# A hybrid encoder step: the first softmax within the projections, and the order of ACT's weight casts among the experts

## The chip, the cores and the metric

The kernel runs on one core of one Trainium2 chip, as one program and one launch. The metric is the device time in microseconds (us). The core has five engines that run side by side and wait for each other through semaphores: TensorE (PE, matmuls), VectorE (DVE), ScalarE (ACT), GpSimd (POOL) and SyncE (SP, which here only issues DMAs). Each executes its own instructions strictly in order.

## The reference, cut to what matters

One layer of a streaming encoder, in float32, for 1024 prompt frames with 16 meta tokens ahead and 8 samples of 16 frames:

```python
h = rms_norm(x)
z_pool, q, k, v, qi, ki, wi, ga, gb = split(h @ w_in)        # q, k, qi, ki are rotated
score  = sum_h(relu(qi @ ki.T) * wi)                          # the 256 best keys of each query are kept
logits = (q @ k.T) * HEAD_DIM ** -0.5, masked to those keys
o = softmax(logits) @ v                                       # 8 heads, 2 key heads, 4 query heads on each
x = x + (sigmoid(ga) * pool_branch(z_pool) + sigmoid(gb) * (o @ w_attn_out)) @ w_out
h = rms_norm(x)
# 32 experts in 4 groups; each token goes to 2 experts of one group
act = silu(h @ w_g[e]) * (h @ w_u[e])
x = x + sum_e(comb[e] * (act @ w_d[e]))
y = rms_norm(x)
```

## The kernel before, in words

**Numbers in two parts.** Most products are made from a high part (the cast of a float32 to the faster type, made by ACT) and a rest (number minus high part, made by DVE or POOL). Three products, high by high, high by rest and rest by high, stand for one float32 product.

**Projections.** The columns of w_in are taken in 19 pieces (`PIECES`), each staged by SP, cast by ACT (`split_hi`), its rest made by POOL or DVE (`split_lo`). The last four pieces are the queries. They are done by `nat_run(RUN_Q)` (PE L923, ACT L1399, POOL further on): 36 tiles of 128 tokens by 256 columns. Turn i of that loop projects tile i on PE (`proj_nat`, 24 products), ACT copies it out (L1338), POOL rotates it, and three turns later (`LAG`) PE transposes it (`trans`, L917) and ACT copies it into `qT` (L1396). PE uses banks 0 to 3 for projections and 4 and 5 for transposes. Meanwhile DVE picks the 256 best keys (`rounds`, L1795 and L1800) and writes the mask; semaphore `selected` tells of it.

**Attention.** The prompt's groups `PG` are 8 query tiles by 2 key heads, the longest first: `PG[0]` is tile 7 with key head 0, `PG[1]` the same tile with key head 1. A group has 4 heads; each head's logits are made in up to three chunks (`qk`, three products of up to 348 columns, L1004, L1007 and L1010, into bank n % 3). DVE takes a chunk, adds the mask and keeps the maximum (`ttr`, L1837), reduces the chunks' maxima (L1842, L1846), ACT takes the exponential (`expo`, L1502), DVE divides by the sum (`scale`, L1850 and L1852). Then PE transposes the probabilities (`p_trans`, L1032), ACT copies them out (`tevac`, L1512), and PE multiplies by the values (`p_values`, L1045). Step st of the loop over `STEPS` (-1 to 15) transposes and multiplies group st while it makes the logits of group st + 1. `plan(st)` sets which chunks stand between which transposes. Step -1 is the logits and softmax of `PG[0]` alone. Before it, PE, ACT and DVE wait for all projections (`pj_done`, `tr_evac`), ACT casts the first queries (L1528) and the keys of both key heads (L1535, six casts), DVE makes the rests of key head 0 and POOL those of key head 1 (L2284).

From step 6 on each step also holds one of the 8 samples: its logits end step st, and step st + 1 ends with `s_values`: five transposes of its probabilities (L1058, L1061), two copies out by ACT (L1514, L1516) and 20 products (L1070).

**Experts.** SP loads the weights of expert e (gate, up, down, 512 KB each, `load_e`, L784 to L786) into one of 7 slots; from expert 7 on it waits until expert e - 7 has left its slot (`dn_done`). Experts 4 to 6 are loaded behind a wait for the first gathered rows (`hg_in[0]`), and behind them SP stores and reads back a small overflow table (L809 to L813). POOL gathers each expert's rows (L2308) three experts ahead and scatters the results (L2313). For each expert PE does: `gate_up_split(e)` (L1238 to L1242), `e_trans(e + 1)` (L1210), `down_of(e - 1)` (L1223), `turn_act(e)` (L1248). ACT does: `silu_e` (L1625), `rows_upper(e + 1)` (L1639), `expert_upper(e + 2)` (two casts of weights, L1631 and L1632, behind a wait for the weights), the copy of the turned product `actT` (L1666), `second_half(e - 1)` (half of the results, L1646). DVE does: the product `act_rows` (L2051), `rows_lower(e + 1)` (L2035), `first_half(e - 1)` (L2042), `expert_lower(e + 2)` (L2028).

## Time and profile before

| | us |
|---|---|
| median of 3 runs (1361.68 to 1365.5) | 1362.36 |
| the profiled execution, its own time | 1362.2 |
| its span in the profile | 1360.2 |
| PE busy / DVE busy / ACT busy / POOL busy | 1280.9 / 925.5 / 500.7 / 478.8 |
| last query projection ends | 611.7 |
| first transposes of probabilities | 629.3 |
| attention's steps end, output projections begin | about 854 |
| experts, from the first transposes of rows to the last results | 1113 to 1311 |

Times inside the execution are counted from the start of the span. A busy share is no measure of what an engine costs: it has to be read where the next step waits.

### The profile page before, as it was taken

The numbers are of one execution on the slowest core, as the hardware profiler recorded it, in microseconds if no ns is written. First come the engines' busy times: TensorE is split into PE (matmuls) and PEld (weight loads), VectorE is DVE, ScalarE is ACT, GpSimd is POOL, SyncE is SP. The second block draws the span as 40 slices with busy tenths as digits, with TensorE's granted clock in tenths as the row PEclk, the third lists the DMA queues.
The fourth block names the chain that finished last, engine by engine and source line by source line (L and its number), as shares of the span: only waits on it lengthen the run. The fifth ranks groups of instructions, "written<-read, shape, count | busy, mean of one in ns | idle before, by whom it ended". The sixth has DMA issues, their size and how long they took to land.

```text
span 1360.2 us, 21285 instructions
## 1 busy us (share of the span) xinstructions
PE 1280.9 (94%) x7533; PEld 1100.8 (81%) x7533; DVE 925.5 (68%) x2189; ACT 500.7 (37%) x1071; POOL 478.8 (35%) x766
## 2 busy tenths in 40 slices
PE   5999999999989999997999989999999979999986
PEld 5999999999979999996666656999788848777742
DVE  5665888888999989816767656233565658767736
ACT  5654222122121122225556444100322237666533
POOL 5801595778882127541000000120011233333314
PEclk9999999999999999998999999899999989999998
DMA  7201232222213222003000220844321248999857
GB/s 254 72 24 44 87 75 78 39 74 57 63 58 113 66 91 56 2 1 98 1 16 1 66 73 25 291 150 163 124 78 49 77 170 335 351 343 341 302 198 311
DMA packets 79312, 163.78 MB, mean 120 GB/s; under 512 B 12529, under 2 KB 47937, under 8 KB 78065
## 3 DMA queue, kind: packets, MB, share of 16 engines
q1 hardware_dynamic: 65121, 129.31, 27.8%
q0 software_dynamic: 12656, 27.62, 6.1%
q10 hardware_dynamic: 1440, 5.58, 1.0%
q8 instruction: 60, 0.98, 0.3%
q14 instruction: 35, 0.29, 0.1%
HBM read 137.81 MB, written 39.21 MB: 130 GB/s over the span
## 4 chain that ended last, share of the span: by engine, by line
PE 77%; DMA 8%; POOL 5%; DVE 3%; ACT 3%; issue 2%; SPq 0%; ACTq 0%; POOLq 0%; DVEq 0%
PE bank L845 11%; PE bank L844 11%; PE bank L846 11%; PE bank L1045 5%; DMA region_h<-in_wd 4%; PE bank L1116 3%; PE bank L1110 3%; PE bank L1032 3%; PE bank L969 2%; PE bank L1128 2%; PE bank L1127 2%; PE bank L1129 2%; PE bank L1223 2%; DMA region_w<-in_wd 2%; PE bank L1112 2%
## 5 line engine op out<-in xcount | busy, mean ns | idle before, releaser
L1795 DVE MAX8 small<-region_kv 128x8 f32<-128x272 f32 (+4 forms) x241 | 190.2, 828 | 47.6 <-DVE region_kv L1800 47.5
L844 PE MATMUL bank<-h_hi,w_hi 128*128 128x384 f32 (+1 forms) x576 | 196.2, 341 | 0.0
L845 PE MATMUL bank<-h_lo,w_hi 128*128 128x384 f32 (+1 forms) x576 | 196.1, 340 | 0.0
L1800 DVE MATCH_REPLACE8 region_kv<-small,region_kv 128x272 f32<-128x272 f32 (+4 forms) x241 | 195.5, 818 | 0.0
L846 PE MATMUL bank<-h_hi,w_lo 128*128 128x384 f32 (+1 forms) x576 | 194.5, 338 | 0.0
L2116 POOL TENSOR_TENSOR w_lo<-w_stage,w_hi 128x512 fp32r<-128x512 f32 x64 | 80.8, 1295 | 144.7 <-ACT w_hi L1327 144.6
L844 PE MATMUL bank<-w_hi,h_hi 128*128 128x256 f32 x448 | 129.2, 288 | 2.3 <-ACT region_q L1390 2.3
L846 PE MATMUL bank<-w_hi,h_lo 128*128 128x256 f32 x448 | 125.9, 281 | 0.0
L845 PE MATMUL bank<-w_lo,h_hi 128*128 128x256 f32 x448 | 125.9, 281 | 0.0
L846 PEld LDWEIGHTS bank<-h_hi,w_lo 128*128 128x128 f32 x576 | 108.8, 189 | 0.0
L845 PEld LDWEIGHTS bank<-h_lo,w_hi 128*128 128x128 f32 x576 | 108.2, 188 | 0.6
L844 PEld LDWEIGHTS bank<-h_hi,w_hi 128*128 128x128 f32 x576 | 108.0, 188 | 0.5
L1045 PE MATMUL bank<-region_t,region_kv 128*128 128x512 f32 (+1 forms) x176 | 88.0, 605 | 2.4 <-ACT region_t L1512 2.4
L844 PEld LDWEIGHTS bank<-w_hi,h_hi 128*128 128x128 f32 x448 | 84.2, 188 | 2.6 <-ACT region_q L1390 2.5
L846 PEld LDWEIGHTS bank<-w_hi,h_lo 128*128 128x128 f32 x448 | 84.4, 189 | 0.0
L845 PEld LDWEIGHTS bank<-w_lo,h_hi 128*128 128x128 f32 x448 | 84.4, 188 | 0.0
L1484 ACT ACTIVATE region_q<-bank 128x384 f32<-128x384 f32 x48 | 23.6, 492 | 159.6 <-PE bank L846 159.6
L2313 POOL DMA_INDIRECT expert_rows_scratch<-region_t,small_i x32 | 35.2, 1100 | 120.9 <-ACT region_t L1646 85.0
L2275 POOL COPY region_h<-region_q 128x128 f32<-128x128 f32 x8 | 2.4, 294 | 190.9 <-PE bank L1070 190.9
L1116 PE MATMUL bank<-o_hi,wao_lo 128*128 128x384 f32 x192 | 69.0, 359 | 0.0
L1110 PE MATMUL bank<-o_hi,wao_hi 128*128 128x384 f32 x192 | 66.2, 345 | 1.5 <-DVE o_lo_prompt L1867 1.5
L1512 ACT COPY region_t<-bank 128x512 f32<-128x512 f32 (+1 forms) x88 | 50.0, 575 | 47.8 <-PE bank L1032 47.8
(307 smaller groups left out, 3179.5 us busy)
## 6 DMA issues: line engine op xcount, KB each, us to landing
w_stage<-in_w_in SPq DMA_DIRECT2D x72, 256.0 KB, 3.2
region_kv<-in_xa SPq DMA_DIRECT2D x16, 512.0 KB, 5.8
region_q<-in_wg SPq DMA_DIRECT2D x12, 512.0 KB
region_q<-in_wu SPq DMA_DIRECT2D x12, 512.0 KB
region_q<-in_wd SPq DMA_DIRECT2D x12, 512.0 KB
region_w<-in_wg SPq DMA_DIRECT2D x10, 512.0 KB
region_w<-in_wu SPq DMA_DIRECT2D x10, 512.0 KB
region_w<-in_wd SPq DMA_DIRECT2D x10, 512.0 KB
```

What stands on the lines that cost most here:

```text
L844: mm(out, st_hi(k), mv_hi(k), start=(k == 0), stop=False)
L845: mm(out, st_hi(k), mv_lo(k), start=False, stop=False)
L846: last = mm(out, st_lo(k), mv_hi(k), start=False, stop=(k == KD - 1))
L1032: last = nc.tensor.transpose(bank[3 + t % 2][0:rows, r * P:(r + 1) * P], probs_of(x, r)[:, k0:k0 + rows], ident)
L1045: last = mm(bank[5 + slot_of(x)][:, :], vS[0:rows, j, g * HD:(g + 1) * HD], PT[0:rows, t % 3, :], start=(j == 0), stop=(j == nb - 1))
L1110: mm(out, hi, o_hi[:, k, c0:c1], start=(k == 0), stop=False, skip_group_check=True)
L1116: last = mm(out, lo, o_hi[:, k, c0:c1], start=False, stop=(k == KD - 1), skip_group_check=True)
L1512: cp(PT[0:rows, t % 3, :], bank[3 + t % 2][0:rows, :]).then_inc(a_te, 1)
L1795: nc.vector.max(m8[:, q, :], x).then_inc(dve_c, 1)
L1800: nc.vector.match_replace(x, m8[:, q, :], x, TAKEN).then_inc(dve_c, 1)
L2116: tt(w_lo(n)[:, kk * m:kk * (m + 1), :], stage(s if s < KD else s % 4, kk, wd), w_hi(n)[:, kk * m:kk * (m + 1), :].bitcast(F32), ALU.subtr ...
L2313: pool.indirect_dma_start(out=y_d, out_offset=bass.IndirectOffsetOnAxis(ap=idx, axis=0), in_=src, in_offset=None, bounds_check=2 * TOK - 1 ...
```

## The change

Five edits:

1. The logits, softmax and casts of `PG[0]` move from step -1 into `nat_run(RUN_Q)`. PE makes two chunks after each of turns 31 to 36, of which turn 35 holds the last projection. ACT casts in turn 29 and takes the four exponentials in turns 33, 34, 36 and 37. DVE starts as soon as its selection is done. Since the memory of the key and query parts still holds projection data, `PG[0]` has buffers of its own, and its logits use banks 6 and 7 in turn (two, not three). The keys of head 1 are cast in turn 36, after the last projection, and those of head 0 are copied to their lasting place in step 0 (three more copies on ACT).
2. The counts of `qk_high` move with it (`high_at`).
3. The samples' transposes are taken out of `s_values` and put before the last two `p_values` of the step (`s_trans`).
4. Among the experts ACT's `expert_upper(e + 2)` stands behind the copy of `actT` and `second_half(e - 1)`.
5. SP no longer waits for `hg_in[0]` before it loads experts 4 to 6.

```diff
@@ SP
             sp.dma_start(heads[:, :, :], lists[0:P, :, :]).then_inc(lidx_in, 16)
-            sp.wait_ge(hg_in[0], 16)
             for e in range(4, NSLOT):
                 load_e(e)
@@ banks, buffers and turns
+        PB_FIRST = [RW[:, 4096 + 1040 * r:4096 + 1040 * (r + 1)] for r in range(3)] + [RW[:, 0:1040]]
+        def logits_bank(x, n):
+            return bank[6 + n % 2] if x == PG[0] else bank[n % 3]
+        FIRST_AT = {31 + j: [(q // 3, q % 3) for q in (2 * j, 2 * j + 1)] for j in range(6)}
@@ PE, nat_run
                     if i >= LAG:
                         trans(run[i - LAG])
+                    if first is not None:
+                        for q, m in FIRST_AT.get(i, []):
+                            first(PG[0], q, m)
@@ PE, qk
-                if n >= 3:
+                if x == PG[0]:
+                    if n >= 2:
+                        pe.wait_ge(a_sm, n - 1)
+                elif n >= 3:
                     pe.wait_ge(a_sm, n - 2)
@@ PE, the samples
+            def s_trans(x, part):
+                pb, t = probs_of(x, 0), T_AT[x]
+                if part == 0:
+                    pe.wait_ge(a_p, U_AT[x] + 1)
+                    pe.wait_ge(a_te, t - 1)
+                    for j in range(4):
+                        last = nc.tensor.transpose(bank[3 + t % 2][:, j * P:(j + 1) * P], pb[:, j * P:(j + 1) * P], ident)
+                    last.then_inc(a_t, 1)
+                else:
+                    pe.wait_ge(a_te, t)
+                    nc.tensor.transpose(bank[3 + (t + 1) % 2][0:32, 0:P], pb[:, 512:SK], ident).then_inc(a_t, 1)
@@ PE, the steps
+            nat_run(RUN_Q, qk)
...
-            for st in STEPS:
+            for st in STEPS[1:]:
...
                 for j in range(max(nb - 2, 0), nb):
+                    if st - 1 in S_STEP:
+                        s_trans(S_STEP[st - 1], j - (nb - 2))
                     p_values(PG[st], j)
@@ ACT
-            act.wait_ge(pj_done, NU)
+            def first_group_steps(i):
+                if i == 29:
+                    act.wait_ge(w_lo_done, W_AT[NPC])
+                    act.wait_ge(pj_done, W_LAST[NPC - 2])
+                    act.wait_ge(tr_evac, RI["q", 1, 9] + 1)
+                    q_upper(PG[0])
+                    for m, (c0, c1) in enumerate(KEY_CHUNKS):
+                        cp(k_hi_first[m][:, :], kT[:, 0, c0:c1]).then_inc(qk_high, 1)
+                if i in (33, 34, 36, 37):
+                    expo(PG[0], (33, 34, 36, 37).index(i))
+                if i == 36:
+                    act.wait_ge(pj_done, NU)
+                    for c0, c1 in KEY_CHUNKS:
+                        cp(k_hi[:, 1, c0:c1], kT[:, 1, c0:c1]).then_inc(qk_high, 1)
+                if i == 37:
+                    act.wait_ge(tr_evac, RI["q", 3, 8] + 1)
+                    q_upper(PG[1])
+
+            nat_run(RUN_Q, first_group_steps)
             act.wait_ge(tr_evac, len(ROPED))
...
                     tevac(PG[st], j)
+                    if st == 0 and j == 3:
+                        for m, (c0, c1) in enumerate(KEY_CHUNKS):
+                            cp(k_hi[:, 0, c0:c1], k_hi_first[m][:, :]).then_inc(qk_high, 1)
@@ ACT, experts
                 if e + 1 < NE:
                     rows_upper(e + 1)
-                if e + 2 < NE:
-                    expert_upper(e + 2)
                 act.wait_ge(act_turned, e + 1)
                 if e >= 2:
                     act.wait_ge(dn_done, e - 1)
                 cp(actT[:, e % 2, :], bank[6 + e % 2][:, 2 * P:3 * P]).then_inc(actT_ready, 1)
                 if e >= 1:
                     second_half(e - 1)
+                if e + 2 < NE:
+                    expert_upper(e + 2)
@@ DVE
-            dve.wait_ge(pj_done, NU)
-            nc.vector.memset(zero, 0.0).then_inc(zero_ready, 1)
-            dve.wait_ge(zero_ready, 1)
             dve.wait_ge(selected, NT)
+            dve.wait_ge(w_lo_done, W_AT[NPC])
+            dve.wait_ge(pj_done, W_LAST[NPC - 2])
...
-            for st in STEPS:
+            for r in range(REP):
+                ttr(PG[0], r)
+                if r >= 1:
+                    scale(PG[0], r - 1)
+            scale(PG[0], REP - 1)
+            dve.wait_ge(pj_done, NU)
+            nc.vector.memset(zero, 0.0).then_inc(zero_ready, 1)
+            dve.wait_ge(zero_ready, 1)
+            q_rest(PG[1])
+            for st in STEPS[1:]:
```

## Rows read from the trace of the kernel before

**Rows 1.** Stage of experts: PE, PEld, DVE, ACT, POOL, clock, DMA share, GB/s
```profile
1184.00:1311.00 127.00, 117.22 (x731) 90.65 (x730) 86.11 (x117) 76.60 (x139) 38.73 (x39) 1.00 0.81 297
```

**Rows 2.** Timeline of PE, 611 to 632: start, us, engine, line, operation
```profile
611.38 0.28 PE L846 MATMUL bank<-w_hi,h_lo 128*128 128x256 f32 x1
...
617.22 0.32 PE L1004 MATMUL bank<-keys_hi,queries_hi 128*128 128x344 f32 x1
617.38 0.32 PE L1007 MATMUL bank<-keys_hi,o_hi 128*128 128x344 f32 x1
...
618.93 0.49 PE L1004 MATMUL bank<-keys_hi,queries_hi 128*128 128x348 f32 x1
...
629.27 1.02 PE L1032 MATMUL bank<-consts,region_t 128*16 128x128 f32 x4 [4.41 <-DVE region_t L1852]
```

**Rows 3.** Timeline of ACT, 611 to 632
```profile
615.08 2.39 ACT L1535 CAST keys_hi<-region_kv 128x348 fp32r<-128x348 f32 x6
...
618.00 1.28 ACT L1502 ACT_TABLE_LOAD   x1
...
626.96 1.16 ACT L1502 ACTIVATE region_t<-region_t,small 128x1040 f32<-128x1040 f32 x1 [1.30 <-DVE small L1846]
```

**Rows 4.** Timeline of DVE, 602 to 632
```profile
611.79 0.28 DVE L1871 MEMSET region_h<- 128x272 f32 x1 [26.19 <-PE bank L846]
...
626.03 0.51 DVE L1837 CUSTOM_DVE_ANT_0 region_t<-bank,region_kv 128x344 f32<-128x344 f32 x1
...
628.45 0.76 DVE L1852 TENSOR_SCALAR region_t<-region_t,small 128x1040 f32<-128x1040 f32 x1
```

**Rows 5.** Granted clock after the gap, in 2 us windows (columns as in Rows 1)
```profile
634.00:636.00 2.00, 2.00 (x9) 1.17 (x7) 1.11 (x6) 0.78 (x2) 0.00 (x0) 0.81 0.03 8
```

**Rows 6.** Timeline of POOL, 611 to 632
```profile
617.16 2.71 POOL L2284 TENSOR_TENSOR keys_lo<-region_kv,keys_hi 128x348 fp32r<-128x348 f32 x3 [3.59 <-ACT keys_hi L1535]
```

**Rows 7.** Waits of PE, 612 to 1100: total us, times, longest
```profile
PE bank L1070 <- ACT region_t L1516: 6.8, 8, 1.2
```

**Rows 8.** Timeline of PE in a step with a sample
```profile
794.30 1.13 PE L1045 MATMUL bank<-region_t,region_kv 128*128 128x512 f32 x2 [1.38 <-ACT region_t L1512]
```

**Rows 9.** Issues of SP, 1088 to 1300: start, us taken, line
```profile
1112.48 0.33 SPq L784 DMA_DIRECT2D region_q<-in_wg  x1
...
1133.38 0.36 SPq L784 DMA_DIRECT2D region_w<-in_wg  x1
```

**Rows 10.** Waits of SP's queue, 1080 to 1320
```profile
SPq L812 <- DMA overflow_table_scratch<-small_i: 13.8, 1, 13.8
...
SPq L784 <- DMA region_t<-ffn_input_scratch,small_i: 8.5, 1, 8.5
```

**Rows 11.** Timeline of POOL, 1088 to 1130: the first gather
```profile
1107.18 1.93 POOL L2308 DMA_INDIRECT region_t<-ffn_input_scratch,small_i  x1 [4.69 <-DVE small_i L2019]
```

**Rows 12.** Chain that ended last, 1085 to 1190: start, us, what
```profile
1135.04 10.31 DMA region_t<-ffn_input_scratch,small_i
```

**Rows 13.** DMA share behind the overflow table (columns as in Rows 1)
```profile
1130.00:1135.00 5.00, 5.00 (x37) 4.27 (x36) 4.03 (x6) 3.43 (x7) 1.98 (x2) 1.00 0.55 143
```

**Rows 14.** Timeline of DVE among the experts
```profile
1151.54 0.29 DVE L2051 TENSOR_TENSOR region_t<-region_t,bank 128x128 f32<-128x128 f32 x1 [0.27 <-ACT region_t L1625]
...
1154.49 2.35 DVE L2028 TENSOR_TENSOR expert_rest<-region_h,expert_high 128x1024 fp32r<-128x1024 f32 x2
1157.11 0.29 DVE L2051 TENSOR_TENSOR region_t<-region_t,bank 128x128 f32<-128x128 f32 x1 [0.27 <-ACT region_t L1625]
```

**Rows 15.** Timeline of ACT among the experts
```profile
1178.49 1.05 ACT L1631 CAST expert_high<-region_q 128x1024 fp32r<-128x1024 f32 x1 [3.05 <-DMA region_q<-in_wd]
...
1298.09 1.05 ACT L1631 CAST expert_high<-region_w 128x1024 fp32r<-128x1024 f32 x1 [1.59 <-DMA region_w<-in_wd]
```

**Rows 16.** Timeline of PE among the experts
```profile
1180.70 1.98 PE L1223 MATMUL bank<-region_w,region_t 128*128 128x512 f32 x4 [0.67 <-ACT region_t L1666]
...
1182.62 0.35 PE L1238 MATMUL bank<-expert_high,rowsT_hi 128*128 128x256 f32 x1
```

More of the change, by code:

```diff
@@ L183, in build @@
             e_high[0] = slots_w.enter_context(nc.sbuf_tensor("expert_high0", [P, 2, KD, P], F32R))
+        with ExitStack() as first_group:
+            first_group.enter_context(nc.sbuf_tensor("first_probs", [P, 1040], F32))
+            q_hi_first = first_group.enter_context(nc.sbuf_tensor("first_queries_hi", [P, REP, P], F32R))
+            k_hi_first = [None] * 2 + [first_group.enter_context(nc.sbuf_tensor("first_keys_hi2", [P, 344], F32R))]
+            first_group.enter_context(nc.sbuf_tensor("first_more_probs", [P, 7216 - 1896], F32))
+            for m in range(2):
+                k_hi_first[m] = first_group.enter_context(nc.sbuf_tensor(f"first_keys_hi{m}", [P, 348], F32R))
         RW = sb("region_w", [P, 8192])
@@ L485, in high_at @@
         def high_at(n):
-            return 1 if n == 0 else 2 * len(KEY_CHUNKS) + n + 1
+            return [1, 2 * len(KEY_CHUNKS) + 2][n] if n < 2 else 3 * len(KEY_CHUNKS) + n + 1
         def rest_at(n):
@@ L918, in trans, with nat_run @@
                 last.then_inc(tr_done, 1)
-            def nat_run(run):
+            def nat_run(run, first=None):
                 for i in range(len(run) + LAG):
@@ L1003, in qk @@
                         pe.wait_ge(qk_high, 3 * nq + m + 2)
-                    mm(out, qh[:, r, :], k_hi[:, g, c0:c1], start=True, stop=False)
+                    keys = k_hi[:, g, c0:c1] if nq else k_hi_first[m][:, :]
+                    mm(out, qh[:, r, :], keys, start=True, stop=False)
                     if r == 0 and m == 0:
                         pe.wait_ge(qk_low, rest_at(nq))
-                    mm(out, lo, k_hi[:, g, c0:c1], start=False, stop=False)
+                    mm(out, lo, keys, start=False, stop=False)
                     if nq < KVH and r == 0:
@@ L1048, in p_values @@
                     last.then_inc(a_o, 1)
[L1050 to L1061 removed]
+            def s_trans(x, part):
[9 more added lines that the diff above has]
+                    nc.tensor.transpose(bank[3 + (t + 1) % 2][0:32, 0:P], pb[:, 512:SK], ident).then_inc(a_t, 1)
+            def s_values(x):
+                i, t, ob = x[1], T_AT[x], bank[7]
                 if i >= 1:
@@ L1397, in evac_tr, with nat_run @@
                        bk[:, 0:256].rearrange("p (j t) -> p j t", j=2)).then_inc(tr_evac, 1)
-            def nat_run(run):
+            def nat_run(run, first=None):
                 for i in range(len(run) + LAG):
@@ L1407, in nat_run @@
                         evac_tr(run[i - LAG])
+                    if first is not None:
+                        first(i)
             def relus(s0, s1):
@@ L1836, in ttr @@
                     add = sc[i][:, c0:c1] if kind == "p" else zero[:, 0:c1 - c0]
-                    nc.vector.tensor_tensor_reduce(out=probs_of(x, r)[:, c0:c1], in0=bank[n % 3][:, 0:c1 - c0], in1=add,
+                    nc.vector.tensor_tensor_reduce(out=probs_of(x, r)[:, c0:c1], in0=logits_bank(x, n)[:, 0:c1 - c0], in1=add,
                                                    scale=1.0, scalar=MASKED, op0=ALU.add, op1=ALU.max,
```

27 lines of the change are left out of this document (6 added, 21 removed).

## The prediction

> **What bounds the kernel now.** I read the busy shares by stage first. PE does nearly all there is to wait for: what the change can win lies where PE is idle or where something else sets its pace. Three such places are touched.
>
> The first is the change-over from projections to attention. In the timeline of PE the last query product starts at 611.38 and ends at 611.66, and the first transposes of probabilities start at 629.27, behind a wait of 4.41 us for DVE [rows 2]. The reader is to see that in these 17.6 us PE only makes the 12 chunks of the first group. The rest is a chain: casts on ACT, a table load, four rounds of maximum, exponential and division [rows 3, 4].
>
> The second are the samples: eight times PE waits for ACT between a sample's transposes and its products, 6.8 us in all [rows 7].
>
> The third is the expert stage. DVE's products of two experts stand 5.57 us apart where nothing is late [rows 14], but from about 1178 on ACT's cast waits for weights every time, and the casts of experts 12 and 31 are 119.6 us apart [rows 15]: 19 steps, 6.29 us each. PE is busy for 117 of 127 us, the 16 DMA engines move 297 GB/s with a tail in which nothing is loaded [rows 1]. So late weights, not PE, set this pace.
>
> **Part 1, the first softmax: 7.4 us.** A chunk is three products that start 0.16 us apart at the full clock [rows 2], 0.48 us. Turns 31 to 34 hold eight chunks, so the last projection ends 3.8 us later, at 615.5; call it T. The other four follow it. After T: two transposes (some 0.2 us), chunk 8 done at T + 0.7, chunk 9 at T + 1.2. DVE takes chunk 8 (0.5), needs 0.4 from its last chunk to the maximum (from 626.03, the chunk's 0.51 us included, to ACT's exponential at 626.96 it is 0.93) [rows 3, 4], divides head 1 (0.9) and takes chunk 9 only then, to T + 3.1. With two banks, chunk 11 has to wait for that: done at T + 3.6, its maximum at T + 4.55. The exponential and the division behind it took from 626.96 to 629.21 [rows 3, 4], 2.3 us. So PE's first transposes start at T + 6.9 = 622.4 in place of 629.27: **6.9 us**.
>
> On ACT this order holds: head 2's exponential (to T + 3.0), three casts of the second keys (half of 2.39 us [rows 3], to T + 4.2), the last exponential at T + 4.55. The table load of 1.28 us [rows 3] falls into turn 33; PE's four banks and the three turns of lag cover it, and if they did not it would cost its 1.3 us. DVE was idle for 26.19 us before 611.79 [rows 4], so its selection ended at 585.6, before turn 29: nothing new waits for it. The three extra copies in step 0 (1.2 us of ACT) stand behind one copy out, in a step where a turn of PE takes over 2 us; without that cover they would cost 1.2.
>
> Then the clock. The matmuls at 618.93 take 0.49 us in place of 0.32 [rows 2], and after the idle stretch PE works at 1.2 GHz until about 635.2, as the granted 0.81 of the window 634 to 636 shows [rows 5]. That is 5.9 us at half rate, some 2.9 us lost. The new gap is shorter but not empty: PE works for about 1 of the 5 us before its restart. Bounds: nothing regained, or all 2.9. I take 1.0, nearer to the end that the drop at 618 shows, which came after less than 5 us of such idling.
>
> What is late next: POOL's rests of the second keys, which still start when the last transpose is out and take 2.71 us for three [rows 6]. They were ready before PE; now PE needs them one by one within that time: 0.5 us lost (0 to 1.5). DVE's memset of 0.28 us [rows 4] and the query rests end at the same time. Sum: 6.9 + 1.0 - 0.5 = 7.4, bounds 5.5 and 9.3.
>
> **Part 2, the samples: 5.7 us.** Two value products of 0.5 us and more now stand between the transposes and the products that need them, so ACT's copies are hidden. In six of the eight steps the wait stood directly behind the transposes: 6 x 0.8 = 4.8. In two steps PE also waits before the value products (1.38 us at 794.30 [rows 8]); the first transposes fit into that, 0.45 each. In the other two steps ACT's own last exponential ends last, and nothing is won. The later steps hang on a chain of DVE and ACT, but that starts at the sample's logits, which PE makes after these products, so it moves up as a whole. Bounds: 2.4 (three long steps alone) and 7.7.
>
> **Part 3, SP's wait: 2.2 us.** SP waited 8.5 us for the first rows and loaded experts 4 to 6 from 1112.48; then it waited 13.8 us for the overflow table's store, which stood behind that load in its queue, so expert 7 was loaded at 1133.38 [rows 9, 10], though its slot came free at about 1125.6. Meanwhile the DMA engines were busy for 0.55 of the time at 143 GB/s [rows 13]. Now loads 4 to 6 start 8.4 us earlier, the table is through before slot 0 is free, and load 7 starts 7.8 us earlier. Of these 7.8 us the gathers and scatters that had the engines for themselves take some 2.6; **5.2** remain, if the rest of the stage stays bound by weights.
>
> Against this stands the first gather, issued at 1107.18 + 1.93 [rows 11] and landed at about 1112.4: 3.3 us without company. The nearest row with company, a gather issued behind loads of three experts, took 10.31 us [rows 12], which would put everything behind it 6.4 to 7 us later. But that one had a scatter ahead of it in its own queue, this one has nothing. I take 3.0 (0.5 to 6.4). 5.2 - 3.0 = 2.2, bounds -1.2 and 4.7.
>
> The Trainium skill ("DMA: Bandwidth & Descriptors", section "Queues, rings and completion order") says that each DMA engine takes turns between its queues, a packet at a time, so that a lone gather should not sit behind a whole backlog. By that rule the delay would be near the low bound; the row speaks for the high one, and no row shows the lone case.
>
> **Part 4, ACT's order: 0.7 us.** With late weights, arriving at t, the two casts, the copy and the half result went before PE's down product: cast at 1178.49, down at 1180.70, next gate product at 1182.62 [rows 15, 16], t + 4.1. Now the down product no longer waits; the gate product waits for casts (1.05 each), DVE's second rest (half of 2.35 [rows 14]) and its product, t + 3.8. The slot comes free 0.9 us earlier. In a stage bound by weights this counts once, at the end, 0.4; I add 0.3 for fuller queues. Bounds -1 and 2.5. Where nothing is late the casts end 2.3 us later and DVE's next product 1.1 later; it had about 2 us until PE turns it, so 0.9 is left.
>
> **Sum.** 7.4 + 5.7 + 2.2 + 0.7 = 16.0. The profiled execution took 1362.2 (span 1360.2 and 2.0 around it), the median of the runs is 1362.36. 1362.2 - 16.0 = **1346.2**.
>
> **Rivals.**
> - *The queues and the clock are kind* (0.20): the gather is late by 0.5 only, +2.5, and the clock comes back at once, +1.9: 1341.8. For it: the skill's rule above. Against: the dropped clock after a similar gap.
> - *The first rows are late* (0.18): the gather takes 10.3 us as in [rows 12], part 3 gives -1.2: 1349.6.
> - *The chains of ACT and DVE keep the samples' gain* (0.12): part 2 gives 2.4, and half-rate matmuls last as long as before, part 1 gives 6.4: 1350.5.
> - *Slower: the casts come too late on DVE* (0.04). Place: DVE's product of each expert, now behind rests that wait for the later casts. The slack of 0.9 us was worked out, not seen. Each expert that overruns it by x costs x, 31 times; from x = 0.5 on the change is slower than before. At 0.7: 1346.9 + 21.7 = 1368.6. Against: DVE works for 4.7 of 5.57 us.
> - *The turns don't do what they say* (0.02): if the new waits held the first chunks back until the projections are over, part 1 would shrink to 1: 1352.6.
>
> **Numbers.** My forecast, within 3 us, has 0.44. The range takes in the kind and the late case and the samples' one: 1340 to 1353. A measurement of this kernel tells 0.3%, 4.1 us, from no change. Faster by over that: 0.95; within: 0.02; slower: 0.03.
>
> **What would show it.** Last projection ends near 615.5, first probabilities transposed near 622.4, clock below 1.0 for under 5 us behind it. No wait of PE before L1070 except in two steps. SP's load of expert 7 issued near 1126 to 1129 and the first rows landed at 1115 or so, counted without the gain ahead of them. Last weights cast some 15 us earlier than 1298.09. The forecast is wrong if PE stalls in the last turns of the projections, if the experts' pace where nothing is late is above 5.57, or if the first gate product comes over 5 us late.

## The result and the profile after

The changed kernel takes 1354.16 us in the median of 6 runs (1351.77 to 1357.88), the kernel before 1362.69 (1361.68 to 1365.5). The ratio is 0.9939, with a 95% interval of 0.9922 to 0.9955: 8.3 us faster, where 16.0 were forecast. The direction was right, the size was not, and the time lies 1.2 us above the range. The profiled execution of the changed kernel is one of its slower ones, 1357.17 us with a span of 1355.3, so its trace shows a little less gain than the median.

All lines of code are numbered by the kernel that a row comes from. PE in the changed kernel, around the last projections (start, us, engine, line, operation, idle time before and its releaser):

```profile
615.98 0.38 PE L932 MATMUL bank<-consts,nbuf 128*128 128x128 f32 x2
...
619.14 0.43 PE L1024 MATMUL bank<-first_keys_hi,first_queries_hi 128*128 128x344 f32 x1 [0.93 <-DVE small L1880]
...
623.25 1.01 PE L1052 MATMUL bank<-consts,region_w 128*16 128x128 f32 x4 [2.93 <-DVE region_w L1895]
...
624.83 0.66 PE L1027 MATMUL bank<-keys_hi,o_hi 128*128 128x348 f32 x1 [0.28 <-DVE o_hi L1920]
```

The last query product ends at 616.14, so T of the forecast is 616.1 (the projections of this execution began 0.65 us later than before). The first transposes stand at 623.25, T + 7.1, where T + 6.9 was forecast, in place of 629.27 [rows 2]. The stall of 0.93 is the one that was forecast for chunk 11 with two banks, and the last 0.28 is a rest of DVE that took 1.35 us beside POOL's rests.

The waits of PE between there and the experts, in total us, times and longest (answers to [rows 7, 8]):

```profile
PE bank L1094 <- ACT region_t L1543: 1.7, 2, 0.9
...
PE bank L1081 <- ACT region_t L1539: 1.3, 2, 0.9
```

The sample's products waited 6.8 us in eight steps and now wait 1.7 in two. But look at the clock there. Windows of the changed kernel; the columns are the busy times of PE, weight loads, DVE, ACT, POOL, then the granted clock, the DMA share and GB/s:

```profile
812.00:816.00 4.00, 4.00 (x19) 2.44 (x20) 1.38 (x5) 0.00 (x0) 0.00 (x0) 0.58 0.00 0
...
840.00:844.00 4.00, 4.00 (x5) 0.96 (x4) 0.00 (x0) 0.58 (x1) 0.00 (x0) 0.50 0.00 0
844.00:848.00 4.00, 2.49 (x9) 2.45 (x9) 1.38 (x2) 0.00 (x0) 0.00 (x0) 0.50 0.33 78
```

0.50 is the level of 1.2 GHz, half of what PE has at 1.00. Twice the missing share, added over the 4 us windows from 612 to 872, gives the time at the lower level: 20.4 us before, 27.2 after. Before, 4.8 of the 20.4 lay in the gap at 616 to 629 and 0.8 in the wait ahead of the output product at 854, where they cost little (in the gap DVE waited twice for chunks of PE, 0.67 us in all). The other 14.8 us lay in work: 8.9 in the steps (629.3 to 634.8, and at 825) and 5.9 in the output projections, as this window of the kernel before shows:

```profile
856.00:860.00 4.00, 4.00 (x14) 4.00 (x14) 0.00 (x0) 2.04 (x2) 1.19 (x1) 0.50 0.99 344
```

After, 3.3 of the 27.2 lie in waits and 23.9 in work.

Then the start of the experts. The timeline of PE in the changed kernel (in these rows a group is cut where the stretch asked for ends):

```profile
1090.27 15.07 PE L1225 MATMUL bank<-consts 128*128 128x512 f32 x28
1107.45 0.74 PE L1237 MATMUL bank<-consts,region_t 128*128 128x128 f32 x5 [2.11 <-DMA region_t<-ffn_input_scratch,small_i]
```

The issues of SP in it:

```profile
1095.11 0.43 SPq L800 DMA_DIRECT2D region_q<-in_wg  x1
...
1100.29 0.65 SPq L824 DMA_DIRECT2D overflow_table_scratch<-small_i  x1
...
1115.36 0.21 SPq L827 DMA_DIRECT2D nbuf<-overflow_table_scratch  x1
...
1121.36 0.37 SPq L800 DMA_DIRECT2D region_w<-in_wg  x1
```

And the first gather in its chain of waits:

```profile
1098.41 8.90 DMA region_t<-ffn_input_scratch,small_i
```

The loads of experts 4 to 6 stand ahead of the gather, as meant. The gather lands 8.90 us after its issue begins, where it was some 5.2 (1107.18 to about 1112.4, [rows 9, 11]); the warming products no longer cover it, and PE is idle for 2.11 us. The overflow table's store still keeps SP for 14 us, and expert 7 is loaded 31.1 us after the start of the warming products, where it was 34.2. The DMA engines run dry behind the early loads (last three columns: clock, share, GB/s):

```profile
1110.00:1115.00 5.00, 4.95 (x31) 4.70 (x30) 0.31 (x2) 1.36 (x4) 0.28 (x1) 0.70 0.46 175
1115.00:1120.00 5.00, 4.38 (x34) 4.17 (x35) 4.11 (x6) 3.60 (x7) 0.99 (x1) 1.00 0.25 65
```

Among the experts, the stage of [rows 1] in the changed kernel:

```profile
1184.00:1311.00 127.00, 116.67 (x706) 88.01 (x704) 81.31 (x111) 74.00 (x130) 44.09 (x38) 1.00 0.79 289
```

The largest wait of PE there:

```profile
PE bank L1275 <- DVE region_t L2102: 9.9, 12, 1.6
```

A late expert on DVE:

```profile
1193.35 2.36 DVE L2079 TENSOR_TENSOR expert_rest<-region_h,expert_high 128x1024 fp32r<-128x1024 f32 x2 [2.85 <-ACT expert_high L1674]
1195.63 0.28 DVE L2102 TENSOR_TENSOR region_t<-region_t,bank 128x128 f32<-128x128 f32 x1
```

And on PE:

```profile
1195.96 0.33 PE L1275 MATMUL bank<-consts,region_t 128*128 128x128 f32 x1 [1.36 <-DVE region_t L2102]
```

DVE's product of an expert stands behind both rests of the next expert, and these wait for the late casts; PE waits for that product before its turn. The last cast [rows 15] comes at 1293.12, 5.0 earlier and not 15.

Where the time went, in one profiled execution of each kernel (us; "between" runs from the first transposes of probabilities to the first output product, "output" from there to the start of the warming products, "head" from there to the first expert's turn, "experts" from the turn of expert 0 to that of expert 31). These executions lie anywhere in the spread of their kernels' times, so their sums are not the medians.

| | first transposes | between | output | head | experts |
|---|---|---|---|---|---|
| before | 629.3 | 224.7 | 245.2 | 19.4 | 188.4 |
| changed | 623.2 | 222.3 | 244.7 | 24.4 | 187.0 |
| first softmax alone | 621.2 | 230.1 | 242.6 | 20.6 | 187.2 |
| samples alone | 631.3 | 221.6 | 245.1 | 20.8 | 186.9 |
| loads alone | 630.8 | 224.7 | 245.2 | 25.3 | 185.9 |
| casts alone | 629.1 | 224.7 | 245.2 | 19.3 | 187.9 |
| changed, no early loads | 622.0 | 218.9 | 241.9 | 20.0 | 188.5 |
| changed, casts as before | 624.4 | 222.3 | 244.8 | 24.4 | 185.7 |
| first softmax and samples | 622.5 | 222.3 | 244.7 | 20.6 | 187.6 |
| changed, samples as before | 623.6 | 232.8 | 244.0 | 24.0 | 186.6 |
| changed, softmax as before | 630.9 | 221.7 | 245.1 | 27.1 | 186.4 |

### The profile page after: what moved, and what is told of

Read it like the earlier page. It is cut to its first block, busy times and chain, and to the rows that moved or that the text cites. A ratio compares the mean times of both kernels' runs of the same rounds, so it can differ in the third digit from the quotient of the medians.

```text
span 1355.3 us, 21293 instructions
## 1 busy us (share of the span) xinstructions
PE 1284.8 (95%) x7533; PEld 1102.7 (81%) x7533; DVE 927.1 (68%) x2189; ACT 505.0 (37%) x1074; POOL 490.2 (36%) x766
## 4 chain that ended last, share of the span: by engine, by line
PE 78%; DMA 8%; POOL 5%; DVE 3%; ACT 3%; SPq 1%; issue 1%; ACTq 0%; POOLq 0%; DVEq 0%
PE bank L860 11%; PE bank L859 11%; PE bank L861 11%; PE bank L1065 5%; DMA region_w<-in_wd 3%; PE bank L1143 3%; PE bank L1052 3%; PE bank L1137 3%; PE bank L987 2%; PE bank L1154 2%; PE bank L1155 2%; PE bank L1156 2%; PE bank L1250 2%; DMA region_h<-in_wd 2%; PE bank L1139 2%; PE bank L1094 2%
## 5 line engine op out<-in xcount | busy, mean ns | idle before, releaser
L1065 PE MATMUL bank<-region_t,region_kv 128*128 128x512 f32 (+1 forms) x176 | 91.0, 614 | 0.0
L1265 PE MATMUL bank<-expert_high,rowsT_hi 128*128 128x256 f32 x256 | 66.2, 295 | 1.5 <-ACT rowsT_hi L1682 1.5
```

Of the source, the lines that this page charges most:

```text
L1065: last = mm(bank[5 + slot_of(x)][:, :], vS[0:rows, j, g * HD:(g + 1) * HD], PT[0:rows, t % 3, :], start=(j == 0), stop=(j == nb - 1))
L1265: mm(out, rowsT_hi[:, par, k, :], high[:, :, k, :], start=(k == 0), stop=False, skip_group_check=True)
```

## The experiments

My theory after the trace: the two parts at the attention are worth what was forecast less what the clock takes, and the early loads cost more at the first gather than they bring. The rivals: the later casts are the loss, or the DMA rate bounds the experts and makes loads and casts worth nothing either way.

**Each part alone.** On the kernel before, first the softmax's move (all that the diff has on it), then the samples' transposes before the last value products of the step, then SP's wait:

```diff
             sp.dma_start(heads[:, :, :], lists[0:P, :, :]).then_inc(lidx_in, 16)
-            sp.wait_ge(hg_in[0], 16)
             for e in range(4, NSLOT):
```

and ACT's order, `expert_upper(e + 2)` moved behind `second_half(e - 1)`.

> The kernel before with the first softmax within the query projections, and nothing else of the change. My prediction's step 1 prices it at 7.4 us (6.9 of tail, 1.0 of clock, less 0.5 for POOL's rests): ratio 0.9946, some 1355.0 us. The changed kernel's first probabilities were transposed at 623.25, 7.1 us after the end of its last query product, so the tail is as forecast. Rival: the half clock that went from 629:635 comes back in the first steps with samples, where the changed kernel's trace has 812:816 at 0.58; then the output product (854.00 before) starts only 3 to 5 us earlier and the ratio is 0.997.

> The kernel before with the samples' transposes dealt before the last value products of the step before, and nothing else. Step 2 prices it at 5.7 us (six steps at 0.8, two at 0.45): ratio 0.9958, some 1356.7 us. Rival, from the changed kernel's trace: the waits of 0.8 us go, but the clock in the steps with samples falls to 0.50 to 0.58 for eight or more us more than before, which costs 2 to 4 us of the gain: ratio 0.997 to 0.999.

> The kernel before with SP's wait for the first gathered rows taken away ahead of the loads of experts 4 to 7, and nothing else. Step 3 prices it at 2.2 us (5.2 for the earlier load of expert 7, less 3.0 for a later first gather): ratio 0.9984. Theory after the changed kernel's trace: the first gather takes 8.9 us where it took about 5, TensorE idles about 2 us and runs the first expert at half clock, so the first turn of the first expert comes about 5 us later against the start of the stage; the loads of experts 8 on come some 8 to 12 us earlier but the DMA rate of 4 to 7 is shared with them. If only the first expert matters: ratio 1.000 to 1.003. If the loads that come earlier shorten the late experts by 5.2: 0.9984.

> The kernel before with ScalarE's cast of the weights of expert e+2 behind the turned product's copy and the second half, and nothing else. Step 4 prices it at 0.7 us: ratio 0.9995. Theory after the changed kernel's trace: TensorE's turn now waits for DVE's product (9.9 us in 12 waits) because the second rest of the weights stands ahead of it in DVE's order and waits for the later cast; where the casts pace the experts this is 0.8 to 1.5 us in each of up to 12 experts, partly in place of the 6.3 us that the wait for the turned copy cost: between 0 and +4 us, ratio 1.000 to 1.003. If the order pays as meant: ratio 0.996 to 0.9995, and the wait for the turned copy (6.3 us in 11) goes.

Measured: the first softmax 0.9977 (0.9965 to 0.9989), 3.1 us; the samples 0.9965 (0.9951 to 0.9978), 4.8 us; the loads 1.0011 (0.9998 to 1.0023), 1.5 us slower, which the interval does not quite part from nothing; the casts 1.0014 (0.9995 to 1.0033), nothing that can be told. The early loads are not worth 2.2 us here; in their trace the head is 6.0 us longer and the experts 2.5 shorter. PE's first transposes of gathered rows with the loads alone:

```profile
1117.76 1.94 PE L1209 MATMUL bank<-consts,region_t 128*128 128x128 f32 x8 [3.30 <-DMA region_t<-ffn_input_scratch,small_i]
```

The window behind them (columns as above):

```profile
1120.00:1125.00 5.00, 4.54 (x24) 4.57 (x25) 0.88 (x2) 1.60 (x2) 0.99 (x1) 0.57 0.48 178
```

SP's issue of the load of expert 7:

```profile
1132.67 0.37 SPq L784 DMA_DIRECT2D region_w<-in_wg  x1
```

PE is idle for 3.30 us, then runs at the lower clock, and expert 7 is loaded at 1132.67, where it was 1133.38 [rows 9]. The forecast had it 7.8 us earlier: it left out that slot 0 comes free only when the late first expert is done.

The first softmax alone starts the transposes 8.1 us earlier, keeps 2.7 of them at the output product and has 5.3 at the warming products. Its clock fell at 761, 795 and 823, in full work, 2 to 3 us behind stalls of 0.81, 0.81 and 0.86 us. The kernel before has the same three stalls at 766, 797 and 823; its clock held behind the first two and fell behind the third. PE with the first softmax alone, at the first of them:

```profile
759.30 0.96 PE L1091 MATMUL bank<-region_t,region_h 128*128 128x64 f32 x7 [0.81 <-ACT region_t L1538]
```

The windows behind it:

```profile
760.00:764.00 4.00, 4.00 (x22) 2.53 (x21) 0.58 (x2) 0.00 (x0) 0.45 (x2) 0.69 0.18 15
764.00:768.00 4.00, 4.00 (x15) 2.77 (x15) 1.75 (x8) 1.30 (x3) 0.00 (x0) 0.50 0.82 262
```

It has 20.6 us at the lower level, as many as before (20.4), but all of them in the steps, where the kernel before has 8.9: "between" is 5.4 longer. In return its output projections start at the full clock, where before they had 5.9 us at half, and "output" is 2.6 shorter. So of the 8.1 us this execution loses some 2.8 to the clock. It is the fastest of its kernel's eight (1356.26, mean clock 0.983; the others 0.977 to 0.981). No trace of a slower one is on record, so where the rest goes, down to the 3.1 us of the ratio, is not shown.

**Each part taken out of the changed kernel,** with the same edits the other way round.

> The changed kernel with SP's wait for the first gathered rows put back ahead of the loads of experts 4 to 7. Alone, taking the wait away cost 1.5 us (ratio 1.0011). If it costs the same beside the other three parts, this kernel is 1.5 us faster than the changed one: ratio 0.9928 to the kernel before. Rival, by the sums (the four parts alone give 4.0, 4.5, -1.5 and -1.9, in all 5, and together 8.3): the early loads pay once casts and samples are changed as well, so this kernel is 1 to 4 us slower than the changed one: 0.995 to 0.997.

> The changed kernel with ScalarE's casts of expert e+2 put back ahead of the turned product's copy and the second half. Alone the later casts cost 1.9 us (0 to 4.5). If that is DVE's product behind the second rest, it is 9.9 us of waits in the changed kernel against 6.3 of the waits that it replaced: this kernel is 2 to 4 us faster than the changed one, ratio 0.991 to 0.9925. Rival: with the loads early the later casts leave the transfers of the next expert sooner or later by nothing, and the difference is within 1 us: 0.993 to 0.995.

> First softmax and samples' transposes alone, on the experts of the kernel before. Alone they were worth 3.1 to 4.0 (0.9977 and 1358.97) and 4.8 (0.9965). If these add: 8 us, ratio 0.994, the same as the changed kernel, and the experts' two parts are worth nothing together. If the changed parts' half clocks add up in the steps with samples (0.58 at 812:816 in the changed kernel): only 5 to 6 us, ratio 0.996, and the experts' two parts together are worth 2 to 3.

> The changed kernel with the samples' transposes back behind the value products. Alone they were worth 4.8 us. If they add: 1359, ratio 0.9975. If the first softmax and they share a loss at the clock (half clock in the steps with samples only where both are in), the part is worth less here, 1 to 3 us: 0.9945 to 0.996.

> The changed kernel without the first softmax's move, the last of the four taken out one by one. Priced at 7.4 us, it gave 3.1 us alone (0.9977) and 5.9 us beside the samples' transposes (0.9965 to 0.9922). If its worth is the tail and the rest is the clock's chance, this kernel is 5 to 7 us slower than the changed one: 0.998 to 0.999. If it is worth only 3 to 4 here: 0.9965.

| kernel | ratio to before | 95% interval |
|---|---|---|
| changed | 0.9939 | 0.9922 to 0.9955 |
| without early loads | 0.9920 | 0.9900 to 0.9939 |
| without later casts | 0.9942 | 0.9920 to 0.9964 |
| without both | 0.9922 | 0.9909 to 0.9935 |
| without the samples' part | 0.9996 | 0.9980 to 1.0011 |
| without the softmax's part | 0.9990 | 0.9977 to 1.0003 |

Two pairs price the early loads (0.9939 against 0.9920, 0.9942 against 0.9922): 2.6 and 2.7 us lost, as alone 1.5. None of the three is clear of its interval by itself; they agree with each other and with the stages (head 3.8 to 6.0 longer, experts 1.5 to 2.5 shorter). So the early loads do shorten the expert stage, whatever the DMA rate is, and lose more in the head. Two pairs price the casts at -0.3 and -0.4 us: nothing. The two parts at the attention give 0.9922 without the other two, 10.6 us of the 13.1 forecast. Taken out one at a time, the samples are worth 7.8 us and the softmax 6.9, more than alone (4.8 and 3.1), in point estimates whose intervals are some 2 us wide to either side.

**The first gather.** Two variants of the changed kernel: 18 warming products in place of 14, and only expert 4's load ahead of the wait:

```diff
-WARM = 14
+WARM = 18
```
```diff
+            load_e(4)
+            sp.wait_ge(hg_in[0], 16)
-            for e in range(4, NSLOT):
+            for e in range(5, NSLOT):
```

> The changed kernel with 18 in place of 14 warming products (36 matmuls) ahead of the experts. In it TensorE is idle for 2.11 us before the first gathered rows and runs the first expert at half clock (0.70 in the mean at 1110:1115). If the clock is a part of the loss, this gives back 1 to 2 us of the changed kernel's time (ratio 0.9925 to 0.993 against 0.9939); if only the late landing counts, nothing changes (0.9939), and the 4 more products end just when the rows land.

> The changed kernel with only the load of expert 4 ahead of SP's wait for the first rows, those of 5 to 7 behind it. If the queue of three loads (4 to 6, 4.7 MB) is what makes the first gather take 8.9 us in place of 5.3, one load costs a third: the gather takes 6 to 7 us, the warming products hide it, and the time is that without early loads or better, ratio 0.9915 to 0.9925. Rival: any load ahead of the gather delays it as much: ratio 0.994 and a wait of about 2 us at the first transposes.

More warming products change nothing: 0.9939 (0.9916 to 0.9962). PE keeps the full clock for the first expert, but its timeline shows that the 36 products take until 1108:

```profile
1089.52 18.53 PE L1225 MATMUL bank<-consts 128*128 128x512 f32 x36
1107.89 1.04 PE L1237 MATMUL bank<-consts,region_t 128*128 128x128 f32 x8
```

The head is 24.1 us, with 14 products 24.4. So the late landing is the main part of the loss, and what the clock returns the longer products take: how the rest divides between the two stays open. One early load gives 0.9919 (0.9896 to 0.9941) and a head of 20.5 us. SP's next load, which waits for the gather issued at 1092.49, starts 4.5 us after it:

```profile
1097.02 0.33 SPq L800 DMA_DIRECT2D region_q<-in_wg  x1
```

So the delay comes with the amount that is queued around the gather, and one load costs and brings nothing that can be told.

**Fewer warming products,** on the kernel without early loads, WARM = 12. There the products end last: they take 14.53 us and stop 1.2 us after the landing at 1096.05, as PE's timeline there has it:

```profile
1082.76 14.53 PE L1226 MATMUL bank<-consts 128*128 128x512 f32 x28
```

> The changed kernel with SP's wait put back (0.992), and 12 in place of 14 warming products (24 matmuls). Without the early loads these products end 0.5 us (before), 1.3 and 2.0 us after the first rows have landed, the more the longer they run at half clock. If they are the limit there: 0.9 to 1.5 us faster, ratio 0.991. Rival: TensorE's clock then falls at the first transposes, and the first experts run at half clock: ratio 0.993 or more.

0.9903 (0.9880 to 0.9925), head 18.4 for 20.0: the 1.7 us show in the trace, in the ratio they are within the intervals.

**The clock in the steps with samples.** Seven kernels so far with both parts at the attention have "between" at 218.7 to 219.0 (three of them) or at 222.3 (four), and the medians hide it: the kernel without early loads ran at 1346.2, 1347.4 and 1348.3 with a mean clock of 0.982 to 0.984, and at 1353.3, 1354.9 and 1355.5 with 0.976 to 0.978. In the four traces at 222.3 the clock falls behind both stalls that the change left, of 0.90 and 0.84 us, at 809 and 833 (in the changed kernel at 810.6 and 834.7); in the other three it falls behind the first alone. The second fall goes with some 3.4 us of "between", and "output" is longer with it too (244.7 to 244.9 for 241.9 to 244.0). The first try lengthens the distance between a sample's transposes and its products:

```diff
-                if st - 1 in S_STEP:
-                    s_values(S_STEP[st - 1])
                 if st in S_STEP:
                     for m in range(len(chunks_of(S_STEP[st]))):
                         qk(S_STEP[st], 0, m)
+                if st - 1 in S_STEP:
+                    s_values(S_STEP[st - 1])
```

> The changed kernel with SP's wait put back (0.992 of the kernel before), and TensorE's value products of a sample moved behind the logits of the next sample. Theory: the stalls of 0.90 at 808 and 0.84 at 832, which are all that is left in the steps with samples, are what the half clock there begins behind (at 810 to 812 and 836, for 7 to 20 us in these traces); with 1.2 us of logits between the transposes and the value products they go, 1.7 us by themselves and up to 3 to 8 us of time at half clock: ratio 0.986 to 0.990, and a narrower spread than the 1346.2 to 1355.5 of the kernel without this. Rival: the clock falls in these steps whatever TensorE waits for, and only 1.7 us come: 0.9905 to 0.991. Rival: DVE and ScalarE are as late with the next sample's probabilities, nothing changes: 0.992.

0.9946 (0.9931 to 0.9960), 3.5 us slower than without it: a miss. The stall at 809 went, and with it the fall there, but the next probabilities now came late, and PE waits in three new places (0.48 at 770, 0.67 at 781, 0.44 at 820). The second stall only split in two, in PE's timeline:

```profile
832.08 0.66 PE L1078 MATMUL bank<-consts,nbuf 128*128 128x128 f32 x4 [0.71 <-DVE nbuf L1896]
835.70 4.45 PE L1095 MATMUL bank<-region_t,region_h 128*128 128x64 f32 x18 [0.45 <-ACT region_t L1544]
```

The clock is at 0.50 from 836 to 848. The next two are on the kernel with 12 warming products. One fills the wait without taking it away:

```diff
+                if i in (5, 7):
+                    for _ in range(2):
+                        mm(ob[:, P:512], ident, consts[:, 0:384], start=True, stop=True, skip_group_check=True)
                 pe.wait_ge(a_te, t + 2)
```

The other takes it away at its source. ACT's copies of a sample's transposes stood behind the step's last exponential, which waits for DVE's maximum:

```diff
-                for r in (ends[nb - 1] if nb else []):
-                    expo(PG[st + 1], r)
-                for r in [r for r, m in after if m == len(chunks_of(PG[st + 1])) - 1]:
+                late = list(ends[nb - 1] if nb else []) + [r for r, m in after if m == len(chunks_of(PG[st + 1])) - 1]
+                for r in late[:-1]:
                     expo(PG[st + 1], r)
                 if st - 1 in S_STEP:
                     tevac(S_STEP[st - 1], 0)
                     tevac(S_STEP[st - 1], 1)
+                for r in late[-1:]:
+                    expo(PG[st + 1], r)
```

> The kernel with SP's wait put back and 12 warming products (0.9903), and before the value products of samples 5 and 7 two products of 128x384 into unused columns of the sample's bank, 0.6 to 0.8 us of work that nobody reads, in the time in which TensorE waits. It takes away the idle time and not the wait. If the idle time is what the clock falls behind, the half clock at 810 to 820 and 835 to 850 goes and the ratio is 0.986 to 0.989; if the clock falls whatever TensorE does in these waits, 0.990 to 0.991 and half clock in the same places.

> The kernel with SP's wait put back and 12 warming products (0.9903), and in ScalarE's order the two evacuations of the sample's transposes ahead of the last exponential of the step. The two stalls left there (0.90 at 809, 0.84 at 833) wait for these copies, which stand behind an exponential that waits for VectorE's maximum. Theory: the stalls go, 1.7 us, and with them the half clock that began behind them at 810 (7 us in the kernel with 12 products, up to 24 in others): ratio 0.985 to 0.988, with fewer runs at the upper end. Rival: the last exponential is 0.8 us later and its probabilities' first transposes stall instead: 0.990 to 0.991, and the clock falls there.

> As the kernel with the sample's evacuations first, with ScalarE's casts of expert e+2 put back as they were before. The three pairs so far give the later casts +1.9 us alone, and -0.4 and -0.3 us beside other parts: within 1 us of the other, either way, and the waits of TensorE for DVE's product (some 10 us in 12) turn into waits for the turned copy (some 6 us in 11).

Filling the wait, with work that nobody reads and that is longer than the wait, gives 0.9878 (0.9863 to 0.9894), and its five runs lie within 3.1 us where the kernel without it spread over 9.5. PE at 809 in the kernel that fills:

```profile
808.96 1.45 PE L1091 MATMUL bank<-consts 128*128 128x384 f32 x4
810.25 1.95 PE L1098 MATMUL bank<-region_t,region_h 128*128 128x64 f32 x14
```

And the window behind it:

```profile
812.00:816.00 4.00, 4.00 (x31) 2.73 (x31) 2.10 (x11) 0.42 (x1) 0.00 (x0) 1.00 0.00 2
```

Here no wait was saved, only idleness. So in these steps the clock falls behind the idle time and not behind the wait as such. The filling products are also wide (384 columns among products of 64); whether narrow ones would do was not tried. The idle time costs more than its own length: the medians differ by 3.5 us (1350.37 and 1346.88), for 0.9 and 0.8 us of idling. The intervals of the two ratios overlap by a little; the spread of the runs and the clock in the trace point the same way. ACT's order gives 0.9872 (0.9855 to 0.9889); its four runs lie within 1.8 us, though in its trace the stall at 809 and the fall behind it are still there, which points at the second stall as the one that spread the runs. Without the later casts it gives 0.9865 (0.9849 to 0.9882), within 1 us as expected, with PE's waits on DVE's product (11.9 us in 10) against waits for the turned copy and the gathers (6.1 and 4.3).

These orders took away only one of the two stalls; in the step at 809 the last exponential stood in the loop over the key tiles. One more edit takes the exponentials of the last key tile out of the loop as well:

```diff
-                    if j >= 1:
+                    if 1 <= j < nb - 1:
                         for r in ends[j - 1]:
                             expo(PG[st + 1], r)
-                late = list(ends[nb - 1] if nb else []) + ...
+                late = [r for q in ends[max(nb - 2, 0):] for r in q] + ...
```

> The kernel with the sample's evacuations first and the casts as before (0.9865), with the order now changed in every step: in the kernel run so far only the stall at 833 had gone, since in the step at 809 the last exponential stood in the loop over the key tiles; the stall of 0.90 at 809 and the half clock from 810 to 819 were still there. Theory: both go here, 0.9 us of stall and 3 to 4 us of clock: ratio 0.9825 to 0.984. Rival: the clock falls a few us further on whatever is waited for (in the kernel with filling products it fell for 4 us at 836): 0.985 to 0.987.

> The same with 10 in place of 12 warming products (20 matmuls). With 12 they still end 0.6 to 0.9 us after the first rows have landed. If they are the limit: 0.5 to 0.9 us faster than the kernel beside it, ratio lower by 0.0005. Rival: TensorE is now idle for 0.1 to 0.3 us and its clock falls with the first expert: equal, or 1 to 2 us slower.

0.9867 (0.9845 to 0.9889) and, with 10 warming products, 0.9853 (0.9833 to 0.9874). The trace of the first has both stalls and every fall of the clock gone from the steps with samples, and "between" is 214.6 us, the shortest of all. In the trace of the second the clock fell again at 837.5, with the first output product. PE in the first at 809, now with no wait:

```profile
808.88 2.83 PE L1095 MATMUL bank<-region_t,region_h 128*128 128x64 f32 x20
```

And its windows:

```profile
812.00:816.00 4.00, 3.97 (x32) 2.81 (x31) 2.82 (x14) 1.72 (x4) 0.00 (x0) 1.00 0.01 2
...
836.00:840.00 4.00, 2.91 (x17) 2.91 (x18) 1.00 (x2) 0.00 (x0) 0.00 (x0) 1.00 0.44 132
```

The expectation, 0.9825 to 0.984, was missed all the same; the ratio lies where the rival had it. In the median it is no faster than the kernel with one stall left (1344.27 and 1344.46): its runs fall into 1341.8 to 1342.2 at a clock of 0.984 to 0.986 and 1346.4 to 1348.8 at 0.980 to 0.982, so in some executions the clock still fell somewhere, and no trace of such a run is on record. The kernel with 10 warming products is the fastest measured, 1342.88 us, 20.3 below the 1363.17 of the kernel before beside it; PE is idle for 0.54 us before the first transposes and keeps its clock. Against 12 its gain of 1.4 us is within the intervals.

## Why the prediction was right or wrong

**Part 1, the first softmax, 7.4: the tail was right, its worth came short.** T + 6.9 was measured as T + 7.1, the stall of chunk 11 and the late rest were there, and nothing was late in the last turns. With the part in, the first transposes stand at 621.2 to 624.4 in every kernel, without it at 629.1 to 631.3. Yet it gave 3.1 us alone and 6.9 at the most. The step that failed is the term "then the clock, 1.0". It asked only what the half rate behind the gap would do, and put the clock in the later steps at nothing. Behind the gap the half rate lasted 5.1 us in the changed kernel and 6.8 with the part alone, for 5.5 before (to 634.8 by the 0.81 of [rows 5], not to 635.2 as the forecast read it): 0.2 regained, or some 0.6 lost. In the later steps the part alone has 13.8 us at half rate, for 3.4 before, and in the output projections none for 5.9. That was read from one execution of each kernel. Why the clock falls behind other stalls once the stage starts 8 us earlier stays open.

**Part 2, the samples, 5.7: right alone, low beside the first softmax.** 4.8 us alone, 7.5 and 7.8 beside the first softmax, where the upper bound was 7.7. The waits went in six of eight steps and stayed in two, as forecast. What was not forecast is that the two that stayed can cost more than their 1.7 us.

**Part 3, SP's wait, 2.2: wrong in its sign, and the largest miss.** It costs 1.5 to 2.7 us (no pair is clear of nothing by itself, but each is clear of a gain of 2.2), 3.7 to 4.9 away from the forecast. The later gather was priced at 3.0 and took 3.7 (8.9 for 5.2), with the idle time and the half clock behind it the head is 3.8 to 6.0 us longer. The gain was priced at 5.2, from a load of expert 7 issued 7.8 us earlier; counted from the warming products it was 3.1 earlier in the changed kernel and 2.2 in the kernel with this part alone, and the experts got 1.5 to 2.5 shorter. The step that failed is that the load was given its 7.8 us in full: the down product of expert 0, which frees its slot, ended 26.0 us after the start of the warming products before (at 1125.2, where the forecast read 1125.6) and 31.1 after, and these 5.0 us took back most of the 8.2 by which expert 7's load had been late. The two terms were taken for independent, but expert 7's load waits for the slot of expert 0, and expert 0 for the gather that the early loads delay.

The gather took 8.9 us, above the 5.2 without company and below the 10.31 of the row with it, and with one load queued in place of three 4.5. The DMA engines were still busy for 0.96 of the time from 1107.3 to 1110.0, at 379 GB/s, when it had landed at 1107.3: it shared the engines and did not wait for the whole backlog. The Trainium skill ("DMA: Bandwidth & Descriptors", section "Queues, rings and completion order") says that each DMA engine takes turns between its queues, a packet at a time. The trace agrees in that the backlog was not waited for; the time it took lies nearer to the 10.31 than to the 5.2. The middle value taken, 3.0 for 3.7, was about right, and neither end was. The row of 10.31 was misread in one point: at 1135.04 the load of one expert and a third of the next had been issued [rows 9], not three.

**Part 4, ACT's order, 0.7: nothing to be told, within its bounds.** Four pairs give +1.9, -0.4, -0.3 and +1.0 us. The gate product was forecast at t + 3.8 for t + 4.1; where the casts are late, PE waits 9.9 to 11.9 us for DVE's product, about as much as it had waited for the turned copy and the gathers (6.3 and 4.4 in the kernel before). At the late expert shown, the cast starts at 1192.28 and the gate product at 1196.18, t + 3.9. Where nothing is late the pace is 5.57 in both, so the slower rival, an overrun in every expert, did not occur.

**Sum.** 13.1 was forecast for the parts at the attention, 10.6 measured; +2.2 for the loads, some -2.6 measured; 0.7 for the casts, about nothing. 16.0 minus 2.5, 4.8 and 0.4 leaves 8.3, the measured gain. The rival "the first rows are late" named the place, at 1349.6, with -1.2 for part 3; what the range left out was this loss twice as large and a shortfall at the clock at the same time. The bounds of part 1 are mis-added: 6.9 + 0 - 1.5 and 6.9 + 2.9 - 0 are 5.4 and 9.8, not 5.5 and 9.3. That the attention's parts together missed by 2.5 only is in part luck: part 1 alone came 4.3 short, and part 2 beside it 1.8 over.

## What to carry to other kernels

A stall of under a microsecond on TensorE can cost several times its length by the clock that falls behind it, so the last stalls of a stretch can be worth much more than their length: here two of them, 1.7 us in all, brought 3.5 to 5.0 us. Look at the granted clock in windows of a few us behind each. Half clock in a gap costs little, and after the gap is closed the clock may fall elsewhere, in work: a forecast should not book the gap's whole length, and should compare the time at the lower level stage by stage, not as one sum (20.4 and 20.6 us here, with 5.4 us lost in one stage and 2.6 won in the next). Before a transfer is issued earlier, follow what it competes with to the buffer that the next transfer waits for: here the early loads delayed the very expert that frees the slot for the next load.

## What the runs showed that was not expected

- Filling a wait kept the clock up, though the wait stayed: 1.45 us of products that nobody reads, put into a wait of 0.90, made the kernel 3.5 us faster in the median and its runs 3.1 us wide in place of 9.5.
- Not every such stall has this effect: behind the one of 0.81 at 766 in the kernel before the clock stayed at 1.00; behind the same stall at 759 in the kernel with the first softmax alone it fell. A stall of 0.94 to 0.95 us, at 784 to 787 ahead of a transpose and two products of 512 columns, is left in the traces of all later kernels with both parts, and in none of them did the clock fall behind it. Executions of one kernel differ by 9 us, and their mean clock with them (0.984 to 0.976).
- Two copies of 0.56 and 0.25 us on ACT, put ahead of one exponential, took 3.0 to 7.7 us out of the stretch between the first transposes and the output product (214.6 and 215.7 in the two traces with them in every step, 218.7 to 219.0 or 222.3 without), of which 1.7 were PE's waits for them.
